# A DeepNorm encoder block: rsqrt moved to GpSimd, the LayerNorm affine to VectorE, and x1 turned by DMA instead of TensorE

## The reference, cut to what matters

```
proj = x @ w_in                        # 1024 -> q 512 | k 128 | v 128 | u 512 | v_g 512
attn = windowed attention(q, k, v)     # |t-s| <= 128, ALiBi, sink logit; 8 heads, 2 kv heads
sgu  = gelu(u) * (W_s @ LN(gelu(v_g)) + b)       # per chunk of 128 positions, 8 groups
mix  = concat(RMSNorm(attn), RMSNorm(sgu)) @ w_out
x1   = LN1(alpha * x + mix)            # gain ln1_g, bias ln1_b
out  = LN2(alpha * x1 + relu(x1 @ w_ff1)^2 @ w_ff2)    # 1024 -> 4096 -> 1024
```

## Time and profile before

| what | value |
|---|---|
| median of 3 runs | 2795.45 us |
| the profiled execution, its own time | 2794.41 us |
| its span on the slowest core (core 2) | 2792.8 us |
| spans of the 8 cores | 2781.2 to 2792.8 us |
| TensorE matmul busy (PE) | 2645.5 us, 95% of the span |
| TensorE weight load busy (PEld) | 1706.4 us, 61% |
| VectorE busy (DVE) | 1491.9 us, 53% |
| ScalarE busy (ACT) | 1072.5 us, 38% |
| GpSimd busy (POOL) | 955.4 us, 34% |
| bytes moved by DMA | 345.81 MB, mean 124 GB/s |

### The profile page before, as it was taken

One profiled execution on the slowest core, in us unless ns is written; L12 is line 12 of the kernel. 1 busy time (PEld: TensorE's weight loads), 2 busy tenths in 40 slices (PEclk: granted clock), 3 DMA queues, 4 the chain that ended last, 5 costly groups with the idle time before them and its releaser, 6 DMA issues.

```text
span 2792.8 us, 57164 instructions; the slowest of 8 cores (2781.2 to 2792.8 us)
## 1 busy us (share of the span) xinstructions
PE 2645.5 (95%) x20844; PEld 1706.4 (61%) x20844; DVE 1491.9 (53%) x2558; ACT 1072.5 (38%) x2241; POOL 955.4 (34%) x661
## 2 busy tenths in 40 slices
PE   4689999999999999999999998899999999999996
PEld 2357777777677777777777676775444444444442
DVE  5876776767777777677767574111222221233222
ACT  4445555555555555555555452221111110111111
POOL 0333333333343333343333334222343322443332
PEclk8789999999999999999999999999999999999998
DMA  9744323423333433333333225663443434543431
GB/s 264 220 128 111 103 80 100 110 88 96 99 102 86 107 95 92 100 103 88 107 97 102 80 92 133 156 189 121 151 164 138 147 141 153 177 159 136 157 106 76
DMA packets 110134, 345.81 MB, mean 124 GB/s; under 512 B 11680, under 2 KB 11680, under 8 KB 99744
## 3 DMA queue, kind: packets, MB, share of 16 engines
q1 hardware_dynamic: 72208, 199.27, 20.6%
...
## 4 chain that ended last, share of the span: by engine, by line
PE 78%; ACT 6%; DVE 6%; issue 4%; DMA 4%; POOL 2%; DVEq 0%; ACTq 0%; SPq 0%; POOLq 0%
PE psum L836 27%; PE psum L804 23%; PE psum L760 8%; PE psum L659 4%; PE psum L673 4%; PE psum L675 4%; DMA hsc<-arena 2%; PE psum L729 2%; ACT L678 1%; PE psum L716 1%; DVE arena L689 1%; DMA arena<-w_gu 1%; PE psum L665 1%; PE psum L667 1%; PE psum L754 1%
## 5 line engine op out<-in xcount | busy, mean ns | idle before, releaser
L804 PE MATMUL psum<-arena 128*128 128x256 bf16 x8192 | 999.6, 274 | 15.8 <-ACT arena L648 9.8
L836 PE MATMUL psum<-arena 128*128 128x512 bf16 x4096 | 891.5, 379 | 4.5 <-POOL arena L858 2.3
L804 PEld LDWEIGHTS psum<-arena 128*128 128x128 bf16 x8192 | 773.2, 98 | 163.0 <-issue 56.1
L836 PEld LDWEIGHTS psum<-arena 128*128 128x128 bf16 x4096 | 399.5, 98 | 491.0 <-issue 16.6
L809 POOL TENSOR_TENSOR arena<-arena 128x512 bf16<-128x512 f32 x256 | 268.9, 1050 | 699.8 <-ACT arena L807 402.1
L807 ACT ACTIVATE arena<-psum 128x512 f32<-128x512 f32 x512 | 302.8, 592 | 370.7 <-PE psum L804 341.1
L774 POOL TENSOR_TENSOR arena<-arena 128x1024 f32<-128x1024 f32 x128 | 309.2, 2415 | 301.4 <-DVE arena L771 273.3
L843 DVE SCALAR_TENSOR_TENSOR arena<-psum,arena 128x512 f32<-128x512 f32 x128 | 88.3, 692 | 593.2 <-PE psum L836 521.6
L646 ACT ACTIVATE arena<-arena 128x1 f32<-128x1 f32 x320 | 93.3, 293 | 782.4 <-DVE arena L849 660.1
L856 POOL TENSOR_TENSOR arena<-arena 128x1024 f32<-128x1024 f32 x62 | 145.7, 2351 | 558.9 <-ACT arena L853 558.9
L809 DVE TENSOR_TENSOR arena<-arena 128x512 bf16<-128x512 f32 x256 | 214.7, 838 | 173.4 <-ACT arena L807 90.5
...
## 6 DMA issues: line engine op xcount, KB each, us to landing
hsc<-arena SPq DMA_DIRECT2D x256, 256.0 KB, 2.5
arena<-hsc ACTq DMA_DIRECT2D x64, 1024.0 KB, 5.3
arena<-x SPq DMA_DIRECT2D x64, 512.0 KB, 5.5
x1s<-arena SPq DMA_DIRECT2D x64, 512.0 KB, 3.4
arena<-x1s ACTq DMA_DIRECT2D x32, 1024.0 KB, 6.1
out<-arena SPq DMA_DIRECT2D x32, 1024.0 KB, 4.1
arena<-xt POOLq DMA_DIRECT2D x64, 256.0 KB, 5.2
arena<-w_ff SPq DMA_DIRECT2D x32, 512.0 KB, 5.5
```

The source lines that it names most:

```text
L804: R.pe(lambda e, fc=fc, ph=ph, z=z: [e.matmul(ph.ap[:, z * 256:(z + 1) * 256], lhsT=w1q[fc // 4].ap[:, c, (fc % 4) * 128:(fc % 4 + 1) * 12 ...
L836: R.pe(lambda e, s_=s_, q=q: [e.matmul(ps[s_][hf].ap, lhsT=hb[fc // 16].ap[:, fc % 16, s_ * 128:(s_ + 1) * 128], rhs=w2c[fc // 4].ap[:, fc ...
```

## The change

- `rsqrt` becomes two GpSimd operations on the [128,1] column: add eps, then power -0.5 with a constant column `mhalf`. The RMS norms fold the factor 512 into their VectorE multiply.
- LN1 is written as two VectorE operations of 1024 elements, (y - mean) * gain and then * rstd + bias, in place of one VectorE and two GpSimd operations.
- x1 is stored a second time, in bf16, to a new HBM tensor `x1h` by the GpSimd queue (cast in the DMA). `ff1_x` is then one DMA transpose per block on the SP queue, from `x1h` into `x1T`; the load of x1 in bf16, the TensorE transposes and the VectorE copy are gone.
- The square of the second bank moves from GpSimd to ScalarE. There are three `hst` buffers in place of two, each half of a buffer has a name of its own, and the last three tiles use eight buffers that lie in the space of `hT[1]`, which belongs to the second half; a small VectorE memset gates them.
- The last tile of the second half is a function of its own, `ff2_last`: its matmuls are grouped by 128 rows and by half of the columns, gain and bias are two VectorE operations per half, and it is stored in four pieces on two queues. The matmuls before it and their number do not change.

```diff
-    def rsqrt(src_ap, src_buf, eps_buf, scale, lnb, outb):
-        R.act(lambda e: e.activation(out=lnb.ap, in_=src_ap, func=AF.Ln, bias=eps_buf.ap, scale=scale),
-              [src_buf, eps_buf], [lnb], 60, "el")
-        R.act(lambda e: e.activation(out=outb.ap, in_=lnb.ap, func=AF.Exp, scale=-0.5), [lnb], [outb], 1, "el")
+    def rsqrt(src_ap, src_buf, eps, outb):
+        R.pool(lambda e: e.tensor_scalar(out=outb.ap, in0=src_ap, scalar1=eps, scalar2=None, op0=ALU.add), [src_buf], [outb], 50)
+        R.pool(lambda e: e.tensor_tensor(out=outb.ap, in0=outb.ap, in1=mhalf.ap, op=ALU.pow), [outb, mhalf], [outb], 50)
...
-        R.dve(lambda e: e.tensor_scalar(out=yb.ap, in0=yb.ap, scalar1=mv1[p].ap[:, 0:1], scalar2=rstd1[p].ap,
-                                        op0=ALU.subtract, op1=ALU.mult), [yb, mv1[p], rstd1[p]], [yb], 1024, 2)
-        for (cst, aop) in ((G1, ALU.mult), (B1, ALU.add)):
-            R.pool(lambda e, cst=cst, aop=aop: e.tensor_tensor(out=yb.ap, in0=yb.ap, in1=cst.ap, op=aop), [yb, cst], [yb], 1024)
+        R.dve(lambda e: e.scalar_tensor_tensor(out=yb.ap, in0=yb.ap, scalar=mv1[p].ap[:, 0:1], in1=G1.ap,
+                                               op0=ALU.subtract, op1=ALU.mult), [yb, mv1[p], G1], [yb], 1024)
+        R.dve(lambda e: e.scalar_tensor_tensor(out=yb.ap, in0=yb.ap, scalar=rstd1[p].ap, in1=B1.ap,
+                                               op0=ALU.mult, op1=ALU.add), [yb, rstd1[p], B1], [yb], 1024)
         R.dma("sp", lambda e: e.dma_start(out=x1s[m * 128:(m + 1) * 128, :], in_=yb.ap), [yb], [x1_lt[m]], f"x1t{m % 3}", 524288)
+        R.dma("pool", lambda e: e.dma_start(out=x1h[m * 128:(m + 1) * 128, :], in_=yb.ap), [yb], [x1h_lt[m]], f"x1u{m % 3}", 524288)
...
-            R.dma("pool", lambda e, m=m, xbb=xbb: e.dma_start(out=xbb.ap, in_=x1s[m * 128:(m + 1) * 128, :]),
-                  [x1_lt[m]], [xbb], f"x1b{s_}", 524288)
-            R.pe(lambda e, xbb=xbb: [e.transpose(psT.ap[:, c, :], xbb.ap[:, c * 128:(c + 1) * 128], ident.ap)
-                                     for c in range(8)], [xbb, ident], [psT], [128] * 8)
             dst = x1T[i % NX1][s_]
-            R.dve(lambda e, dst=dst: e.tensor_copy(out=dst.ap, in_=psT.ap), [psT], [dst, xgate[i]], 1024, 2)
+            R.dma("sp", lambda e, m=m, dst=dst: e.dma_start_transpose(out=dst.ap, in_=x1h[m * 128:(m + 1) * 128, :]),
+                  [x1h_lt[m]], [dst, xgate[i]], f"x1T{i % NX1}_{s_}", 262144)
...
+        if i == NI - NHXT:
+            R.dve(lambda e: e.memset(nmr1[0].ap, 0.0), [], [hxg, nmr1[0]] + hxw, 1)
         for g in range(8):
-            hs = hst[hn[0] % 2]
-            hkey = f"hst{hn[0] % 2}"
+            if i >= NI - NHXT:
+                j = hn[0] % len(hx)
+                hs, h2, hkey, hg = hx[j], hx2[j], f"hx{j}", [hxg]
+            else:
+                j = hn[0] % NHST
+                hs, h2, hkey, hg = hst[j], hst2[j], f"hst{j}", []
...
-                eng = R.dve if k == 0 else R.pool
-                eng(lambda e, hs=hs, r_=r_, k=k: e.tensor_tensor(out=hs.ap[:, k * 512:(k + 1) * 512], in0=r_.ap, in1=r_.ap,
-                                                                 op=ALU.mult), [r_], [hs], 512)
+                if k == 0:
+                    R.dve(lambda e, hk=h2[k], r_=r_: e.tensor_tensor(out=hk.ap, in0=r_.ap, in1=r_.ap, op=ALU.mult),
+                          [r_] + hg, [h2[k]], 512)
+                else:
+                    R.act(lambda e, hk=h2[k], r_=r_: e.activation(out=hk.ap, in_=r_.ap, func=AF.Square), [r_] + hg, [h2[k]], 480)
...
+    def ff2_last(i):
...
+        for s_ in range(2):
...
+            for hf in range(2):
...
+                for q in range(8):
+                    R.pe(lambda e, s_=s_, q=q, hf=hf: [e.matmul(ps[s_][hf].ap, ...
...
+                R.dve(lambda e, s_=s_, hf=hf, y_=yh[hf]: e.scalar_tensor_tensor(
...
+                R.dve(lambda e, hf=hf, p=p, y_=yh[hf]: e.bn_stats(out=stB[p].ap[:, hf * 6:(hf + 1) * 6], in_=y_.ap), [yh[hf]], [stB[p]], 512)
+            R.dve(lambda e, p=p: e.bn_aggr(out=mvB[p].ap, in_=stB[p].ap), [stB[p]], [mvB[p]], 52)
+            rsqrt(mvB[p].ap[:, 1:2], mvB[p], EPS / (ALPHA * ALPHA), rstdB[p])
...
+                R.dma("sp" if hf == 0 else "act", lambda e, s_=s_, hf=hf, y_=yh[hf]: e.dma_start(
+                    out=out[i * 256 + s_ * 128:i * 256 + (s_ + 1) * 128, hf * 512:(hf + 1) * 512], in_=y_.ap),
+                    [yh[hf]], [], f"outl{s_}{hf}", 262144)
```

More of the change, by code:

```diff
@@ L377, in build_nc @@
     x1s = nc.dram_tensor("x1s", [T, D], F32).ap()
+    x1h = nc.dram_tensor("x1h", [T, D], BF16).ap()
     hsc = nc.dram_tensor("hsc", [NI, 128, 8192], BF16).ap()
@@ L387, in build_nc @@
     x1_lt = [LT(f"x1s{m}") for m in range(NB)]
+    x1h_lt = [LT(f"x1h{m}") for m in range(NB)]
     h_lt = [[LT(f"h{i}_{g}") for g in range(8)] for i in range(NI)]
@@ L465, in build_nc @@
     B1 = A.buf("B1", F32, [D])
-    x1b = [A.buf(f"x1b{i}", BF16, [D]) for i in range(2)]
     x1T_all = [A.alloc(BF16, [8, 256]) for i in range(0)]
@@ L475, in build_nc @@
     rl = [A.buf(f"rl{i}", F32, [512]) for i in range(2)]
-    hst = [A.buf(f"hst{i}", BF16, [1024]) for i in range(2)]
+    NHST = 3
+    hst = [A.buf(f"hst{i}", BF16, [1024]) for i in range(NHST)]
+    hst2 = [[Buf(h_.ap[:, k * 512:(k + 1) * 512], f"hh{i}_{k}") for k in range(2)] for i, h_ in enumerate(hst)]
+    A.cover([b_.lt for h2 in hst2 for b_ in h2])
     W1OFF = A.off
@@ L496, in build_nc @@
     hT[0] = [over(f"hT0_{g}", BF16, [16, 256]) for g in range(2)]
-    hT[1] = [over(f"hT1_{g}", BF16, [16, 256]) for g in range(2)]
+    hT[1] = []
+    hx, hx2 = [], []
+    for g in range(2):
+        ap = A2.alloc(BF16, [16, 256])
+        t = Buf(ap, f"hT1_{g}", extra=A.under(*A2.last))
+        hxgate_w = t.extra
+        flat = ap.rearrange("p a b -> p (a b)")
+        for k in range(4):
+            hx.append(Buf(flat[:, k * 1024:(k + 1) * 1024], f"hx{g}{k}"))
+            hx2.append([Buf(hx[-1].ap[:, z * 512:(z + 1) * 512], f"hx{g}{k}{z}") for z in range(2)])
+            t.extra = t.extra + [b_.lt for b_ in hx2[-1]]
+        hT[1].append(t)
+        hxw.extend(hxgate_w)
     x1r.append(over("x1r0", F32, [2, D]))
@@ L536, in build_nc @@
     R.dve(lambda e: e.memset(epsA.ap, EPS), [], [epsA], 1)
+    R.dve(lambda e: e.memset(mhalf.ap, -0.5), [], [mhalf], 1)
     R.dve(lambda e: e.memset(epsB.ap, EPS / (ALPHA * ALPHA)), [], [epsB], 1)
@@ L687, in sgu @@
         R.dve(lambda e: e.bn_aggr(out=mv[p].ap, in_=st6[p].ap), [st6[p]], [mv[p]], 26)
[L688 removed]
+        rsqrt(mv[p].ap[:, 1:2], mv[p], EPS, rstd[p])
         R.dve(lambda e: e.tensor_scalar(out=vn[p].ap, in0=g.ap, scalar1=mv[p].ap[:, 0:1], scalar2=rstd[p].ap,
@@ L699, in sgu @@
               [sf], [dst, ssq_s[p]], 740)
-        rsqrt(ssq_s[p].ap, ssq_s[p], epsA, 1.0 / 512.0, lnv_s[p], rs_s[p])
-        R.dve(lambda e: e.tensor_scalar(out=dst.ap, in0=sf.ap, scalar1=rs_s[p].ap, scalar2=None, op0=ALU.mult),
+        rsqrt(ssq_s[p].ap, ssq_s[p], 512.0 * EPS, rs_s[p])
+        R.dve(lambda e: e.tensor_scalar(out=dst.ap, in0=sf.ap, scalar1=rs_s[p].ap, scalar2=512.0 ** 0.5, op0=ALU.mult, op1=ALU.mult),
               [sf, rs_s[p]], [dst], 512, 2)
@@ L742, in attention @@
               [af], [attn_n[p], ssq_a[p]], 740)
-        rsqrt(ssq_a[p].ap, ssq_a[p], epsA, 1.0 / 512.0, lnv_a[p], rs_a[p])
-        R.dve(lambda e: e.tensor_scalar(out=attn_n[p].ap, in0=af.ap, scalar1=rs_a[p].ap, scalar2=None, op0=ALU.mult),
+        rsqrt(ssq_a[p].ap, ssq_a[p], 512.0 * EPS, rs_a[p])
+        R.dve(lambda e: e.tensor_scalar(out=attn_n[p].ap, in0=af.ap, scalar1=rs_a[p].ap, scalar2=512.0 ** 0.5, op0=ALU.mult, op1=ALU.mult),
               [af, rs_a[p]], [attn_n[p]], 512, 2)
@@ L897, in build_nc @@
             ff2_load(i + 2)
-        ff2(i)
+        if i < NI - 1:
+            ff2(i)
+        else:
+            ff2_last(i)
     R.emit(nc, es)
```

36 lines of the change are left out of this document (30 added, 6 removed).

## The result

The changed kernel takes 2755 us (2753.5 to 2756.1), 0.986 [0.984, 0.988] of the kernel before: some 40 us faster, where 55 were forecast. In its profiled execution the cores of one die were disturbed, so it is read on core 1, of the other die; means over cores are over undisturbed cores.

The account below looks back on a forecast made before the run. TensorE was taken as the bound in both halves. Transposes 28, change of halves 12, tail 11 and rsqrt 4 sum to 55 us, so 2794.4 becomes 2739 us; the forecast's own range was 2715 to 2765, the full range 2712 to 2790.

Parts of the forecast that it names:

- Tail: End of the kernel, after the last matmul: 20 us would become 9, gaining 11 us, bounds 5 and 12.
- Change of halves: Between first and second half, 1680 to 1820 us: more h buffers would win 12 of 16.8 us idle, bounds 0 and 17.
- Square on ScalarE: ScalarE, per block: four rsqrt leave, four squares come, +0.5 us, counted as nothing; up to 5 us if ReLUs wait.
- TensorE transposes: First half: 64 sets of x1 transposes at 0.44 us leave TensorE, gaining 28 us, bounds 0 and 28.
- rsqrt: Moved to GpSimd at 0.3 to 0.4 us an operation; 4 us of TensorE's 9.8 + 6.0 us waits gained.
- L689: VectorE operation, 1152 ns against 537 for L701: without GpSimd's big products 0.6 us less per block, net effect counted as nothing.
- Start: The first 210 us, where DVE is nearest to full: LN1's affine on DVE may cost or give 8 us.
- No L785 group: Sign of a right forecast: the L785 group is absent from the new profile.
- DVE's wait on `hsc`: Sign near the change of halves: VectorE's wait for h stores, 57.1 us before, would fall below 20 us.
- Rival 1's weak form: Change of halves: h stores land as late as now and its waits stay, 2751 us; chance 0.10.
- Rival 2: GpSimd rsqrt slow, 1.05 us an operation: chain 1.6 us longer, each of 64 blocks stops TensorE, 2841 us; chance 0.12.
- Rival 3: DMA transposes take over 27 us for 128 rows and starve TensorE; at 30 us each, 2931 us; chance 0.03.

## Why the prediction was right, and where it was not

- **The bound.** Right: all gains and losses are TensorE's idle time, its clock, its work, or the tail.
- **Tail, 11 us.** Right: 11.4 in the trace, 12 in the run that undoes it. The rsqrt in it takes 1.15 us (0.22 of L668 and 0.78 of L669, with the step between), 0.35 more than taken.
- **Change of halves, 12 of 16.8 us: this step failed.** Nothing was won there. The prediction set three buffers, which cover two group times, about 7.6 us, against the median landing of an h store, 4.5 us. The longest one counts: it was 12.3 us in the same window of the kernel before (core 2), and after three stores in a row took 16 to 18 us beside the `w_ff2` loads. The second part that it missed is ScalarE's list: it saw that the load of `hT[1]` waits for the last stores, but not that the wait stands ahead of ReLUs. The two runs that remove these waits gain 26 us together. "Square on ScalarE", costed at nothing, waits for the same stores, but it is not the cause: with the square back on GpSimd TensorE stops there too.
- **TensorE transposes, 28 us.** The price is right: from TensorE to DMA, with no products on GpSimd, the mark moves by 1693.1 - 1668.0 = 25 us. But TensorE's busy time fell only from 2640.8 to 2628.4 us (means of the cores 1 to 3), 12 of the 28; the run with the transposes on TensorE and no products has 2659.5 (cores 0, 1 and 3), 19 more than before for the same matmuls in another order. Why an order is dearer by that much was not settled.
- **rsqrt, 4 us.** Its price was taken a little low (0.6 to 0.8 for 0.94), and its effect on the time is nil (2756 with it on ScalarE). The wait behind it on ScalarE, 9.6 us, did go, and another 12 us at the scores and the value product that the prediction did not name went with the rest of the change: steady idle time fell by 17 us in 210 to 1640 us, and by 23 up to the mark, not by 4. At the scores either of the two large edits alone is enough: 1.9 us are left with the DMA transposes alone, 1.7 with the products alone (core 1).
- **L689.** The prediction had the right row (1152 ns beside L701's 537) and booked its 0.6 us as VectorE work that costs nothing. In the kernel before that is nearly so, 5.7 us of waits at the gate. With the transposes off TensorE it is not: 21.5 us at the gate, and 27 us in the time, between the two runs with the rsqrt on ScalarE that differ in GpSimd's products. In the runs that put products back beside the rsqrt, 32 and 53 us, the rsqrt's place in GpSimd's list comes in as well.
- **Start.** TensorE has been busy for 4 us less at 210 us (133.4 against 137.2, means of cores 1 to 3), inside the 8 named.
- **The sum** (cores 1 to 3): 12 less busy time + 23 less idle from 210 us to the mark (37.9 to 14.5) - 4 at the start - 2 behind the mark + 11 tail = 40, measured 41. That the total lies in the forecast range is in part luck: the transposes gave 12 of busy time where 28 were counted and the change of halves nothing where 12 were, and 23 us of steady idle time where 4 were counted made up for them.
- **The signs.** No L785 group, 14.7 us of steady waits, L689 (L710 now) at 550 ns and 8.8 us from the last matmul to the end came as named. DVE's wait on `hsc` (26.2 us, under 20 named), the clock at the change of halves (0.95, near 1.00 named) and the power (0.685 us, under 0.4 named) did not.
- **The rivals.** Rival 1's weak form (2751: the change of halves keeps its waits) is what happened in that place, and its time is nearer than the forecast's. Rival 2 did not come, at 0.94 us for a rsqrt, but it was rated too cheap: it asked 64 us for each us of chain, and the run with a longer chain paid 128/1.32 = 97 at the mark and 207/1.32 = 157 in all, the second half and the clock included. Rival 3 did not come: 3.4 us for 128 rows, and no steady wait of TensorE for `x1h`. By the estimate from the page "VectorE: DVE Perf Modes" of the Trainium skill, section "The three transpose paths", the eight pieces would take 10.5 us; they land in 3.4. The preference for TensorE, which the page gives in its section "Rules for kernel authors", does not hold here, where TensorE is the bound: 2791 against 2756.
